# A two-layer hybrid encoder on one core: feed-forward on the input without the norm's factor, its low parts made by VectorE, the gate half scaled by Pool

## The chip, the cores and the metric

One core of one Trainium2 chip runs the whole kernel. The metric is the device time of one execution in microseconds; the kernel before has a median of 3319.37 us over three runs.

## The reference, cut to what matters

The input, 16 meta tokens and 512 tokens of 1024 channels, passes through two layers. Each layer is a half-step feed-forward, a mixing stage, and a second half-step feed-forward, so that there are four feed-forwards in all. Each sub-layer has an RMS norm ahead of it and one behind it:

```
def _rms_norm(x, g):
    y = xf * lax.rsqrt(jnp.mean(xf * xf, axis=-1, keepdims=True) + NORM_EPS)
    return y * g

def _swiglu(x, w_in, w_out):
    gate, up = jnp.split(x @ w_in, 2, axis=-1)
    return (jax.nn.silu(gate) * up) @ w_out

x = x + 0.5 * _rms_norm(_swiglu(_rms_norm(x, g_pre), w_in, w_out), g_post)
```

`w_in` is 1024 x 5632 (gate and up, 2816 each), `w_out` is 2816 x 1024. The norm's factor, 1/sqrt(mean + EPS), is one number per token. Because only the gate half passes through a nonlinear function, a factor per token left out of the up half multiplies the whole output of that token, and the norm behind removes it, but for its EPS.

## The kernel before, in words

Activations lie with channels on the partitions and tokens along the free dimension: `h` is 128 x 8 x 528. Every product of fp32 numbers is made of three fp32r matmuls: each operand is split in a high part (a copy in fp32r) and a low part (operand minus high part), and high x high, high x low and low x high are summed. So each 128 x 1024 piece of weights needs a high part (ScalarE, line 754) and a low part (a subtraction on VectorE, line 932, or on Pool in two instructions, line 636) before TensorE can use it.

A feed-forward is `phase_ffn` (line 534). It runs in this order.

- **The lead** (`Lead`, lines 340 to 477) finishes the norm behind the sub-layer before: VectorE scales `fo` (line 447) and adds it to `h` (line 450), one of eight channel blocks at a time. ScalarE makes `u_high` = h x gain (line 372) and the squares (line 375), VectorE `u_low` (line 442). The product of the first classical units is computed in the same loop (lines 706 to 719), from h x gain without the norm's factor. The factor `rs` is ready only after the last block: its sums (TensorE, line 417), a reciprocal (line 459) and a root (line 380).
- **The classical units**: the first 2 of 11 pairs of 128-wide blocks (NC = 2) are computed plainly, in four units each (lines 653 to 669), numbered 0 to 7. VectorE multiplies what comes out by `rs`, gate and up (`evac`, line 875), ScalarE applies silu (line 786), VectorE multiplies the two (line 889). Pool makes the low parts of these weights (lines 642 to 645).
- **The pairs 2 to 10** use Strassen's seven products, named A11, A22, A12, S2, S1, S3, S4 in their order on TensorE (`product`, line 671), with the input split in four quarters B11, B21, B22 and B12 and combined in four sums and differences T1 to T4. The inputs to these products are h x gain x rs, made by VectorE (`normalised`, line 894) in the storage of `hidden`, and then split again in high and low parts (`combo_high`, line 797, on ScalarE; `combo_low`, line 904, on VectorE). Every engine runs its queue in order, and the order is written out by hand. In pair p ScalarE has: the high part of product 3's weights; silu of the pair before, over both halves at once (`silu_pair`, line 790, called at line 848); then `s1`, a copy of the bank of A11 (lines 833 to 837); then high parts again. TensorE's third product, A12, accumulates in that bank and waits for `s1` (line 684). VectorE has, at the beginning of pair p: the last two sums of pair p-1 (`c21`, line 956, and `c12`, line 960), a weight's low part, and the product `hidden` of gate and up (line 966).
- **The output product** has 24 units of 8 or 6 weight blocks (line 729), whose low parts Pool makes (line 646). The high and low parts of the hidden tiles 0 to 19 are made during the last pair, those of 20 and 21 after it. `Out` (line 495) copies the result, scales it by the gain and sums its squares for the norm behind.

A ring of R = 4 buffers holds weights and their two parts; a transfer of new weights waits for the low part that last read the buffer (`free`, line 603).

Of the kernel before, what the change touches and what calls it, by code (L numbers as in the profile page):

```python
# [99 lines left out]
def build_program(nc, x, meta_tokens, norm_gain, ffn_w_in, ffn_w_out, w_in, rw_mu, rw_w0, rw_w_up,  # L100
# [4 lines left out]
    with ctx:  # L105
# [234 lines left out]
        class Lead:  # L340
# [6 lines left out]
            def __init__(self, st, ring, pre, banks, later):  # L347
                self.ring, self.pre, self.later = ring, pre, later
                self.rq = sb(st, "rq", [P, 2, 8])
                self.idle = PS[:, banks[2], 0:P]  # L350
# [11 lines left out]
            def scalar(self, act, between=None):  # L362
                nc.scalar.activation(self.rq[:, 0], ones[:, 0:8], ACT.Sqrt).then_inc(S("table"), 1)
# [14 lines left out]
                if self.later:  # L378
                    act.wait_ge(S("recip"), 2)
# [41 lines left out]
            def factor(self, v, own, x):  # L421
# [3 lines left out]
                rq = self.rq[:, x]  # L425
                sums = PS[:, self.bank if x else POST_BANK]
                nc.vector.tensor_scalar(rq[:, 0:full], sums[:, 0:64 * full:64], 1.0 / D_MODEL, EPS, ALU.mult, ALU.add)
                own(nc.vector.tensor_scalar(rq[0:m, full:full + 1], sums[0:m, 64 * full:64 * full + 1], 1.0 / D_MODEL,
                                            EPS, ALU.mult, ALU.add))
                nc.vector.reciprocal(rq, rq).then_inc(S("recip"), 1)  # L430

            def vector(self, v):
                own = Chain(v, S("norm_own"))
                v.wait_ge(S("table"), 1)
# [18 lines left out]
                if self.later:  # L453
                    low(KD - 1)
                v.wait_ge(S("h_summed"), KD)
                if self.later:
                    own(nc.vector.tensor_scalar(halves(rs[:]), self.wide_sums, 1.0 / D_MODEL, EPS, ALU.mult, ALU.add))
                    v.sem_inc(S("sums_read"), 1)
                    nc.vector.reciprocal(rs[:], rs[:]).then_inc(S("recip"), 1)
# [19 lines left out]
        def phase_post_norm(st):  # L479
            lead = Lead(st, None, None, (4, 6, 0), False)  # L480
# [14 lines left out]
        class Out:  # L495
# [6 lines left out]
            def __init__(self, st, gain, scale, done, cut):  # L502
                self.gs = sb(st, "gs", [P, KD])
                self.gain, self.scale, self.done, self.cut = gain, scale, done, cut
# [18 lines left out]
            def add(self, v):  # L523
                for m in range(1, KD - 1):
                    v.wait_ge(S("out_squares"), m + 1)
                    if m == 1 and self.cut.t0:
# [3 lines left out]
                    t = slice(self.cut.t0, T)  # L530
                    nc.vector.tensor_tensor(ssq[:, 2, t], ssq[:, 2, t] if m > 1 else ssq[:, 0, t], ssq[:, m % 2, t],  # L531
                                            ALU.add).then_inc(S("added"), 1)

        def phase_ffn(l, which, pre, gain, cut):

            with ExitStack() as st:
# [8 lines left out]
                ON_POOL = ()  # L545
# [9 lines left out]
                out = Out(st, gain, 0.5, S("unit_done"), cut)  # L555
                lead = Lead(st, [cc[:, 0, 0], cc[:, 0, 1]], pre, (6, 4, 0), True)
# [9 lines left out]
                by_pool = [True] * (4 * NC) + [j in ON_POOL for p in range(NC, NP) for j in range(7)] + [True] * NOUT  # L566
# [9 lines left out]

                def combo(e, h):

                    x = more[:, e, h] if e < 3 else flat((uh, ul)[h][:])[:, 2 * T * (e - 3):2 * T * (e - 2)]
                    return blocks(x[:, 0:4 * n2])  # L580

                plain = lambda x: flat(hid[:])[:, (4 + 2 * x) * T:(4 + 2 * x) * T + 4 * n2]
                OF = {B11: 0, B21: 2, B22: 3, T1: 4, T3: 5, T2: 6, T4: 7}
# [15 lines left out]

                with nc.Block() as block:  # L600
                    @block.sync
                    def _(sp):
# [9 lines left out]

                        for i in range(NP):
                            for q in range(2):
                                if i:
                                    free(i, q)
# [2410 lines left out]
```

## Time and profile before

| | |
|---|---|
| median of 3 runs (lowest, highest) | 3319.37 us (3317.99, 3324.27) |
| the profiled execution: its own time, its span | 3330.05 us, 3328.3 us |
| its mean granted TensorE clock | 0.978 |
| TensorE busy with matmuls | 3184.1 us (96%) |
| VectorE busy | 1905.9 us (57%) |
| ScalarE busy | 1350.7 us (41%) |
| Pool busy | 809.1 us (24%) |

The span runs from the first to the last instruction; the profiled execution's own time is 1.75 us longer. Busy time is the time in which at least one instruction of the engine runs. "Idle before" a group is the time for which the engine did nothing ahead of its instructions, with the instruction that ended the wait behind an arrow. The granted clock is a share of full speed: 1.00 is 2.4 GHz, 0.50 is 1.2 GHz.

The four feed-forwards begin at about 14, 1275, 1668 and 2920 us of the span. In the rows of the trace a time is the start in us from the span's start, followed by the duration in us.

### The profile page before, as it was taken

What the parts mean: (1) busy time and instruction counts of PE and PEld (TensorE: products, weight loads), DVE (VectorE), ACT (ScalarE), POOL (GpSimd) and SP (SyncE); (2) the same over time, 40 slices, a digit from 0 to 9 for tenths busy, and PEclk for the clock granted to TensorE, in tenths of its full rate; (3) what the DMA queues carried; (4) which work ended last, traced back from release to release, by engine and by line L of the source; (5) the groups of instructions that cost most, each with busy time, mean ns of one, the idle gap of its engine ahead of it and who ended that gap; (6) DMA issues with size and microseconds to landing.
All of it is one profiled execution on the core that took longest, in us unless ns stands there. A gap on an engine that the chain in (4) does not pass through costs nothing. (4 is left out here: it accounts for less than half of the span.)

```text
span 3328.3 us, 68766 instructions
## 1 busy us (share of the span) xinstructions
PE 3184.1 (96%) x29414; PEld 2957.0 (89%) x29414; DVE 1905.9 (57%) x2852; ACT 1350.7 (41%) x2277; POOL 809.1 (24%) x618
## 2 busy tenths in 40 slices
PE   8999999999999999999989999999999999989997
PEld 8999999987788999899989999999777778879986
DVE  7884055445767336886078831454467663378832
ACT  3444252224554333444245442523245553335541
POOL 4004335110012443003330043352100125420052
PEclk9999999999999999999999999999899999999999
DMA  3333222002121332333123332220021213223331
GB/s 103 102 102 94 61 75 68 12 3 64 45 52 32 93 93 71 94 109 99 56 94 101 107 89 62 64 62 12 12 61 45 52 42 95 80 82 107 117 91 49
DMA packets 369995, 237.30 MB, mean 71 GB/s; under 512 B 16510, under 2 KB 368012, under 8 KB 369692
## 3 DMA queue, kind: packets, MB, share of 16 engines
q1 hardware_dynamic: 369692, 232.91, 24.3%
q8 instruction: 233, 3.82, 0.5%
q14 instruction: 70, 0.57, 0.1%
HBM read 230.50 MB, written 2.10 MB: 70 GB/s over the span
## 5 line engine op out<-in xcount | busy, mean ns | idle before, releaser
L636 POOL TENSOR_TENSOR W_low<-W,W_high 128x512 fp32r<-128x512 f32 (+1 forms) x256 | 339.4, 1350 | 1192.3 <-ACT W_high L754 1191.8
L155 PE MATMUL PS<-u_high,dW_high 128*128 128x264 f32 (+1 forms) x1344 | 410.1, 305 | 12.9 <-POOL dW_low L2103 8.4
L157 PE MATMUL PS<-u_high,dW_low 128*128 128x264 f32 (+1 forms) x1344 | 386.5, 288 | 0.0
L156 PE MATMUL PS<-u_low,dW_high 128*128 128x264 f32 (+1 forms) x1344 | 386.0, 287 | 0.0
L155 PE MATMUL PS<-u_high,W_high 128*128 128x264 f32 (+1 forms) x1152 | 363.0, 315 | 15.1 <-POOL W_low L636 10.1
L754 ACT ACTIVATE W_high<-W 128x1024 fp32r<-128x1024 f32 (+1 forms) x236 | 241.2, 1027 | 322.6 <-PE PS L157 200.0
L156 PE MATMUL PS<-hidden_low,W_high 128*128 128x264 f32 (+1 forms) x1232 | 369.6, 300 | 0.0
L157 PE MATMUL PS<-u_high,W_low 128*128 128x264 f32 (+1 forms) x1152 | 357.2, 310 | 0.0
L700 PE MATMUL PS<-u_high,W_high 128*128 128x264 f32 (+1 forms) x1152 | 327.4, 284 | 8.3 <-DVE cc L944 8.3
L701 PE MATMUL PS<-u_low,W_high 128*128 128x264 f32 (+1 forms) x1152 | 327.4, 284 | 0.0
L702 PE MATMUL PS<-u_high,W_low 128*128 128x264 f32 (+1 forms) x1152 | 327.3, 284 | 0.0
L155 PEld LDWEIGHTS PS<-u_high,dW_high 128*128 128x128 f32 (+1 forms) x1344 | 257.2, 191 | 37.2 <-issue 18.5
L700 PE MATMUL PS<-u_more,W_high 128*128 128x264 f32 (+1 forms) x864 | 248.3, 287 | 20.9 <-DVE W_low L932 20.9
L531 DVE TENSOR_TENSOR ssq<-ssq 128x528 f32<-128x528 f32 (+1 forms) x36 | 32.3, 897 | 404.9 <-ACT ssq L519 404.9
L156 PEld LDWEIGHTS PS<-u_low,dW_high 128*128 128x128 f32 (+1 forms) x1344 | 257.3, 191 | 1.9
L157 PEld LDWEIGHTS PS<-u_high,dW_low 128*128 128x128 f32 (+1 forms) x1344 | 256.3, 191 | 0.0
L156 PE MATMUL PS<-u_low,W_high 128*128 128x264 f32 (+1 forms) x816 | 256.0, 314 | 0.0
L702 PE MATMUL PS<-u_more,W_low 128*128 128x264 f32 (+1 forms) x864 | 248.3, 287 | 0.0
L701 PE MATMUL PS<-u_more,W_high 128*128 128x264 f32 (+1 forms) x864 | 247.8, 287 | 0.0
L155 PEld LDWEIGHTS PS<-u_high,W_high 128*128 128x128 f32 x1152 | 218.1, 189 | 32.4 <-POOL W_low L636 11.2
L156 PEld LDWEIGHTS PS<-hidden_low,W_high 128*128 128x128 f32 x1232 | 231.6, 188 | 7.8
L2103 POOL TENSOR_TENSOR dW_low<-dW,dW_high 128x512 fp32r<-128x512 f32 x102 | 170.6, 1682 | 258.9 <-ACT dW_high L2098 258.7
(445 smaller groups left out, 8528.6 us busy)
## 6 DMA issues: line engine op xcount, KB each, us to landing
W<-in_ffn_w_in SPq DMA_DIRECT2D x176, 512.0 KB, 5.3
dW<-in_w_in SPq DMA_DIRECT2D x172, 256.0 KB, 2.9
W<-in_ffn_w_out SPq DMA_DIRECT2D x64, 512.0 KB, 4.1
W<-in_w_in SPq DMA_DIRECT2D x80, 256.0 KB, 3.0
W<-in_ffn_w_out SPq DMA_DIRECT2D x32, 384.0 KB, 3.4
W<-in_w_branch SPq DMA_DIRECT2D x48, 256.0 KB, 2.8
W<-in_w_out SPq DMA_DIRECT2D x32, 256.0 KB, 2.8
xt<-in_x SPq DMA_DIRECT2D x4, 512.0 KB, 5.4
```

Of the source, the lines that this page charges most:

```text
L155: nc.tensor.matmul(dst, wh, xh, start=first, stop=False)
L156: nc.tensor.matmul(dst, wh, xl, start=False, stop=False)
L157: return nc.tensor.matmul(dst, wl, xh, start=False, stop=final)
L531: nc.vector.tensor_tensor(ssq[:, 2, t], ssq[:, 2, t] if m > 1 else ssq[:, 0, t], ssq[:, m % 2, t], ALU.add).then_inc(S("added"), 1)
L636: ins = g.tensor_tensor(dst, src, high.bitcast(F32), ALU.subtract)
L700: nc.tensor.matmul(dst, wh, xh, start=OPENS[j] and k == 0, stop=False, skip_group_check=True)
L701: nc.tensor.matmul(dst, wh, xl, start=False, stop=False, skip_group_check=True)
L702: last = nc.tensor.matmul(dst, wl, xh, start=False, stop=k == 3, skip_group_check=True)
L754: copy = lambda dst, src: nc.scalar.activation(dst, src, ACT.Copy)
L2103: g.tensor_tensor(self.WL[:, r], self.W[:, r], self.WH[:, r].bitcast(F32), ALU.subtract).then_inc(S("d_split"), 1)
```

## The change

- The seven products of pairs 2 to 10 take h x gain without the factor. The quarters B11, B21 and B22 are now read from `u_high` and `u_low` as the lead made them, so they are not made again; only T1 to T4 are split in high and low parts. The eight unscaled blocks that the sums T1 to T4 need are made by ScalarE (`plain_parts`) between the lead's loop and the root, in place of the eight `normalised` on VectorE.
- In pairs 2 to 10 Pool multiplies the gate half by `rs`, 128 x 2 x 528 elements in one instruction, after `c11`, `c12`, `c21` and `c22` of that pair, and `silu_pair` waits for that. The up half is not scaled. The last pair's multiplication stands in Pool's queue ahead of the low parts of the output's weights.
- In the classical units VectorE multiplies only the gate by `rs`; the up half is read from PSUM by the product itself.
- The low parts of the classical units' weights, and of the first two output units, go from Pool to VectorE.
- The weights of pair 0 come in eight transfers of half the size, the first block's first.
- The low and high parts of the hidden tiles are placed elsewhere in the last pair: four each at its products 2, 4, 5 and 6, and 16 to 19 after it.
- Since the output is now larger by 1/rs, the EPS of the norm behind is multiplied by the mean of the squares (`mean`) and added to the sum of the output's squares, in one VectorE instruction more per feed-forward; the fixed EPS of that norm becomes 0.
- VectorE no longer waits at the beginning of a `Lead` for ScalarE's first table function.

The place of `silu_pair` in ScalarE's queue, between the high part of product 3 and the copy `s1`, is not changed, nor are the waits of A12 or the sums of a pair.

```
-            def scalar(self, act, between=None):
-                nc.scalar.activation(self.rq[:, 0], ones[:, 0:8], ACT.Sqrt).then_inc(S("table"), 1)
+            def scalar(self, act, between=None, after=None):
+                nc.scalar.activation(self.table[:], ones[:, 0:8], ACT.Sqrt)
...
-            def vector(self, v):
+            def vector(self, v, between=None):
                 own = Chain(v, S("norm_own"))
-                v.wait_ge(S("table"), 1)
...
                 for k in range(KD):
                     own(nc.vector.tensor_tensor(fo[:, k], fo[:, k], self.spread, ALU.mult))
+                    if between:
+                        between(k)
...
+                if self.mean is not None:
+                    v.wait_ge(S("out_squares"), 1)
...
+                    nc.vector.scalar_tensor_tensor(out=ssq[:, 2, t], in0=self.mean[:, t], scalar=KD * EPS,
+                                                   in1=ssq[:, 0, t], op0=ALU.mult, op1=ALU.add
+                                                   ).then_inc(S("mean_added"), 1)
...
-                by_pool = [True] * (4 * NC) + [j in ON_POOL for p in range(NC, NP) for j in range(7)] + [True] * NOUT
+                by_pool = [False] * (NIN + 2) + [True] * (NOUT - 2)
...
+                QUADRANT = {B11: (slice(0, 4), first_half), B21: (slice(4, 8), first_half),
+                            B22: (slice(4, 8), second_half), T3: (slice(0, 4), second_half)}
...
+                both_factors = rs[:, t0:T].unsqueeze(1).broadcast_to([P, 2, T - t0])
+                SPLIT_AT = {2: 0, 4: 1, 5: 2, 6: 3}
...
+                        for s in range(2):
+                            for q in range(2):
+                                for t in range(2):
+                                    c = t * D_FF + s * P
+                                    sp.dma_start(quarter(s, q)[:, t], wi[:, 4 * q:4 * q + 4, c:c + P]
+                                                 ).then_inc(landed[2 * q + t] if s else S(f"first_landed{q}"), 16)
...
-                        for i in range(NC):
-                            for s in range(2):
-                                for q in range(2):
-                                    by_set(classical(i, s, q), quarter(s, q))
+                        for p in range(NC, NP):
+                            for name in ("c11", "c12", "c21", "c22"):
+                                g.wait_ge(S(name), p - NC + 1)
+                            g.tensor_tensor(cc[:, 0, :, t0:T], cc[:, 0, :, t0:T], both_factors, ALU.mult
+                                            ).then_inc(S("scaled"), 1)
...
                         def silu_pair(p):
-                            act.wait_ge(S("c12"), p - NC + 1)
-                            act.wait_ge(S("c21"), p - NC + 1)
-                            act.wait_ge(S("c22"), p - NC + 1)
-                            act.wait_ge(S("c11"), p - NC + 1)
+                            act.wait_ge(S("scaled"), p - NC + 1)
                             nc.scalar.activation(cc[:, 0, :, t0:T], cc[:, 0, :, t0:T], ACT.Silu).then_inc(S("silu"), 1)
...
+                        def plain_parts():
+                            for k in range(KD):
...
+                                nc.scalar.activation(dst[:, :, k % 4 * n2:k % 4 * n2 + n2], two(h[:, k, t0:T]), ACT.Copy,
+                                                     scale=lead.gain(k)).then_inc(S("plain"), 1)
...
-                            tt(cut.of(cc[:, 1, s]), ps(1), cut.of(rs[:]), ALU.mult).then_inc(dve_evac, 1)
...
+                            tt(cut.of(hid[:, 2 * i + s]), PS[:, 4 * s + 2:4 * s + 2 + cut.a, 0:cut.n], cut.of(cc[:, 0, s]),
+                               ALU.mult).then_inc(S("hidden"), 1)
+
+                        def classical_low(n):
+                            i, s, q = n // 4, n // 2 % 2, n % 2
+                            v.wait_ge(S("high"), n + 1)
+                            tt(part_of(WL, n % R, n), quarter(s, q), part_of(WH, n % R, n).bitcast(F32), ALU.subtract
+                               ).then_inc(S("low_dve"), 1)
```

## Rows read from the trace of the kernel before

**Rows 1.** TensorE's waits over the whole span (us in total, times, longest us)

```profile
PE PS L700 <- DVE W_low L932: 20.9, 4, 5.9
PE PS L161 <- POOL W_low L636: 11.9, 4, 3.5
...
PE PS L155 <- POOL W_low L636: 10.1, 4, 3.1
...
PE PS L700 <- DVE cc L944: 8.3, 4, 2.3
```

**Rows 2.** Stretches on TensorE: from:to, length, busy, granted clock, DMA share, GB/s

```profile
24.00:94.00 70.00, 62.46 (x440) 0.90 0.25 79
271.00:275.00 4.00, 3.92 (x19) 0.57 0.09 27
1285.00:1354.00 69.00, 60.02 (x438) 0.93 0.25 77
1677.00:1747.00 70.00, 61.01 (x443) 0.93 0.25 81
1923.00:1927.00 4.00, 3.40 (x15) 0.57 0.01 4
2930.00:3000.00 70.00, 62.36 (x263) 0.90 0.28 89
```

**Rows 3.** ScalarE in order of time, at the beginning of one pair

```profile
175.88 1.09 ACT L795 ACTIVATE cc<-cc 128x1056 f32<-128x1056 f32 x1 [1.83 <-DVE cc L964]
176.88 0.60 ACT L754 ACTIVATE s<-PS 128x528 f32<-128x528 f32 x1
```

**Rows 4.** VectorE in order of time, in the same pair

```profile
175.15 0.70 DVE L964 TENSOR_TENSOR cc<-cc,PS 128x528 f32<-128x528 f32 x1
175.76 1.22 DVE L932 TENSOR_TENSOR W_low<-fo,W_high 128x1024 fp32r<-128x1024 f32 x1
```

**Rows 5.** TensorE in order of time: first matmuls of the third and fourth product

```profile
178.61 0.28 PE L700 MATMUL PS<-u_more,W_high 128*128 128x264 f32 x1
...
181.51 0.28 PE L700 MATMUL PS<-u_high,W_high 128*128 128x264 f32 x1
```

**Rows 6.** The beginning of the first feed-forward, all engines in order of time

```profile
21.43 2.95 POOL L636 TENSOR_TENSOR W_low<-W,W_high 128x512 fp32r<-128x512 f32 x2 [9.46 <-ACT W_high L754]
...
23.18 1.76 DVE L450 TENSOR_TENSOR h<-h,fo 128x528 f32<-128x528 f32 x1
...
24.52 0.36 PE L161 MATMUL PS<-u_high,W_high 128*128 128x264 f32 x1 [2.40 <-POOL W_low L636]
...
26.50 0.70 DVE L450 TENSOR_TENSOR h<-h,fo 128x528 f32<-128x528 f32 x1
...
82.25 2.01 ACT L754 ACTIVATE W_high<-W 128x1024 fp32r<-128x1024 f32 x2 [6.82 <-DMA W<-in_ffn_w_in]
```

**Rows 7.** Groups of Pool by shape: count | busy us, mean ns of one | idle before

```profile
L636 POOL TENSOR_TENSOR W_low<-W,W_high 128x256 fp32r<-128x256 f32 x32 | 23.5, 736 | 0.0
...
L1695 POOL TENSOR_TENSOR normed<-h,rs 128x528 f32<-128x528 f32 x16 | 20.8, 1300 | 23.0 <-POOLq L169 21.9
```

**Rows 8.** VectorE and Pool in order of time, 478 to 492 us

```profile
478.77 5.34 DVE L1381 TENSOR_TENSOR_SCAN rw_s<-rw_s 128x2112 f32<-128x2112 f32 x1 [0.22 <-DVE pj_rw L1367]
...
482.40 2.81 POOL L2103 TENSOR_TENSOR dW_low<-dW,dW_high 128x512 fp32r<-128x512 f32 x1 [2.70 <-ACT dW_high L2098]
...
486.74 3.23 DVE L1383 TENSOR_TENSOR rw_s<-rw_s 128x2112 f32<-128x2112 f32 x1
...
488.77 2.33 POOL L2103 TENSOR_TENSOR dW_low<-dW,dW_high 128x512 fp32r<-128x512 f32 x1 [1.02 <-ACT dW_high L2098]
```

**Rows 9.** TensorE after the second and fourth wait for L944; columns as in rows 2

```profile
1531.23 0.39 PE L700 MATMUL PS<-u_high,W_high 128*128 128x264 f32 x1 [2.00 <-DVE cc L944]
...
1532.00:1536.00 4.00, 4.00 (x35) 1.00 0.27 83
3171.00:3175.00 4.00, 4.00 (x36) 1.00 0.32 92
```

More of the change, by code:

```diff
@@ L340, in build_program, with __init__ @@
         class Lead:
-            def __init__(self, st, ring, pre, banks, later):
-                self.ring, self.pre, self.later = ring, pre, later
+            def __init__(self, st, ring, pre, banks, later, post_eps=EPS, mean=None):
+                self.ring, self.pre, self.later, self.post_eps, self.mean = ring, pre, later, post_eps, mean
                 self.rq = sb(st, "rq", [P, 2, 8])
+                self.table = sb(st, "table", [P, 8])
                 self.idle = PS[:, banks[2], 0:P]
@@ L378, in scalar @@
                 if self.later:
+                    if after:
+                        after()
                     act.wait_ge(S("recip"), 2)
@@ L495, in build_program, with __init__ @@
         class Out:
-            def __init__(self, st, gain, scale, done, cut):
+            def __init__(self, st, gain, scale, done, cut, mean=None):
                 self.gs = sb(st, "gs", [P, KD])
-                self.gain, self.scale, self.done, self.cut = gain, scale, done, cut
+                self.gain, self.scale, self.done, self.cut, self.mean = gain, scale, done, cut, mean
             def gains(self, v):
@@ L761, in classical_high @@
                             n = classical(i, s, q)
-                            for t in range(2):
-                                act.wait_ge(landed[2 * q + t], 16 * (i + 1))
+                            if i == 0 and s == 0:
+                                act.wait_ge(S(f"first_landed{q}"), 32)
+                            else:
+                                for t in range(2):
+                                    act.wait_ge(landed[2 * q + t], 16 * (i + 1))
                             ring(n)
@@ L985, in _ @@
                         combination(6, 3, 4)
-                        multiplied(0, 1)
                         v.wait_ge(S("combos"), 3)
                         combination(7, 2, 6)
-                        for e in range(3):
-                            combo_low(e)
-                        evac(1, 0)
+                        gate(0, 1)
+                        classical_low(6)
+                        classical_low(7)
+                        multiplied(0, 1)
+                        combo_low(T4)
+                        combo_low(T2)
+                        combo_low(T1)
                         sums(NC, S1)
+                        sums(NC, S2)
+                        gate(1, 0)
+                        sums(NC, S3)
                         multiplied(1, 0)
-                        sums(NC, S2)
-                        sums(NC, S3)
                         sums(NC, S4)
@@ L1041, in _ @@
                         c12(NP - 1)
+                        for k in range(16, KF - 2):
+                            hidden_low(k)
                         hidden(NP - 1)
@@ L2961, in ffn @@
             def ffn(which, gain, cut):
-                phase_ffn(l, which, G_NORM + KD * 4 * which, gain, cut)
+                phase_ffn(l, which, G_NORM + KD * 4 * which, gain, cut, EPS if which or l == 0 else 0.0)
             ffn(0, G_NORM + KD, WHOLE)
```

175 lines of the change are left out of this document (94 added, 81 removed).

## The prediction

> **What bounds the kernel now.** I read the page first: TensorE is busy for 96% of the span, so whatever does not shorten or lengthen its waits costs nothing. The change removes no matmul. The next view is therefore the list of TensorE's waits. Its four largest entries inside the feed-forwards, four waits each, are for low parts of weights made by VectorE (20.9 us), for low parts made by Pool (11.9 and 10.1 us) and for a sum of VectorE (8.3 us): 51.2 us in 16 waits [rows 1]. All four belong to the beginning of a feed-forward, but for the last, which falls in the last pair of blocks. The second thing to see is the granted clock of the same stretches [rows 2]: behind these waits it falls to its lower level, 1.2 GHz of 2.4. What was lost is (1 - granted share) x length: 7.0, 1.7, 4.8, 4.9, 1.7 and 7.0 us, together 27.1 us. Third, one pair of the steady part (20.4 us, nine in each of four feed-forwards) on ScalarE, VectorE and TensorE [rows 3 to 5]. There TensorE never waits; I read it for how late each helper may be.
>
> **What the change does at the beginning of a feed-forward.** The first low part takes Pool 2.95 us in two instructions, and TensorE starts at 24.52 after 2.40 us of idleness [rows 6]. Afterwards VectorE makes it in one instruction of 1.22 us [rows 4] and the first weights come in half-size transfers, so TensorE starts some 2.2 us earlier. VectorE also no longer runs against Pool: its addition of h took 1.76 us beside a Pool instruction and takes 0.70 without one [rows 6]. The eight products h x gain x factor leave VectorE for ScalarE, where they lie before the root of the sums; ScalarE was idle there. Three high and three low parts of the input are not made at all, because u_high and u_low now serve as they are. So the low parts of classical units 4 to 7 are done before TensorE comes to them, and the transfer of the first pair's weights, which was so late that ScalarE waited 6.82 us for it up to 82.25 [rows 6], is issued over 10 us earlier by my walk, as soon as the low parts of units 6 and 7 free the buffers. SP's queue gets four transfers more ahead of the parameter loads, which are needed only at the feed-forward's end. I take all twelve waits of the beginning as gone. In the last pair the low parts of the hidden tiles move behind the sum that the sixth product needs, so that wait (8.3 us in four) goes too.
>
> A wait costs 0.16 us more than the idle time listed, since a matmul lasts 0.28 us but its successor starts 0.12 us after it [rows 5]: (181.51 - 178.61)/24 = 0.12. Gain: 51.2 + 16 x 0.16 + 27.1 = 80.9 us. What is late next: 0.2 us at the first product; 0.5 at the fifth step of the lead, where VectorE has 1.2 us of a low part more; in the first pair the second product waits for the hidden tile made from the last classical unit (the gate product, table function and product, 0.70 each, start late behind three low parts: 4.2 us after the unit, with 2.9 of cover, so 1.3). With 0.1 at unit 3 that is 2.1 us in each of four. At the end of a feed-forward Pool's queue holds the last scaling ahead of the low parts of output unit 2. I walk it to 1.5 us too late, and half of these waits bring down the clock at 1.7 us each: 4 x 1.5 + 2 x 1.7 = 9.4. So 80.9 - 8.4 - 9.4 = 63. VectorE no longer waits for ScalarE's table at seven beginnings, 0.15 us each: 1. **Gain in all: 64 us.** The extra VectorE addition (mean times EPS, one per feed-forward, 0.7 us as its neighbours) lies beside output products; if TensorE did not cover it, it would cost 4 x 0.7.
>
> **What it adds in each pair.** Until now the gate half went from VectorE's last sum (175.15 to 175.85) straight to ScalarE: table function at 175.88, then in the same queue the copy of the first product, s1, from 176.88 to 177.48 [rows 3, 4]. The third product accumulates in the bank that this copy reads, and waits for it; it starts at 178.61 [rows 5], 1.13 us after the copy. The change puts Pool's multiplication between the sum and the table function, and leaves table function and copy in their order. Behind the waiting table function stand the copy and a weight's high part, and for the copy waits TensorE.
>
> Pool's instruction reads 128x1056. Undisturbed it took 1.30 us for 128x528 and 0.74 for 128x256 [rows 7], so 1056 take 1.30 + 528 x 0.56/272 = 2.39. But at 175.76 VectorE starts a low part from two SBUF operands, 1.22 us long [rows 4], 0.17 us before Pool can start. Two rows show what that does: Pool's 128x512 (1.27 by the same slope) took 2.81 with 1.71 us of such a VectorE instruction still to run, and 2.33 with 1.20 [rows 8]. It ends later by what is left less 0.15. Here 1.05 is left: 2.39 + 0.90 = 3.29. From both sides the price is 2.39 (no hindrance) to 3.6 (the whole 1.22 added, nothing overlapped); I take 3.29 as the rows nearest to it give it.
>
> Walk: sum done 175.85, Pool starts 175.93 and ends 179.22, the table function starts 0.14 later (the step that TensorE shows behind Pool at 24.52 [rows 6]), the copy 1.00 after it [rows 3] and ends 180.96; product three starts at 181.01, not 178.61. **2.4 us** are lost. They don't come back: VectorE's chain to the last sum hangs on TensorE's fifth product, so it shifts along and the next pair has the same offset. Pairs that have such a predecessor: 8 in each of 4 feed-forwards, 32. 32 x 2.4 = 77 us.
>
> The clock: four waits of about 2 us for VectorE's sum stood alone in a dense stretch. Behind the first and third of them the clock was 0.57 over 4 us [rows 2], behind the second and fourth it stayed at 1.00 [rows 9]. A fall costs 0.43 x 4 = 1.7 us. The new idle time is 2.4 - 0.16 = 2.24 us, so I take 0.6 falls per wait (bounds 0 and 1): 32 x 0.6 x 1.7 = 33 us.
>
> **Sum.** 77 + 33 - 64 = +46 us. The sum is made against the profiled execution (span 3328.3, time 3330.05, so 3376 for it); that run stood 10.7 us above the median of the three, to which the same difference is applied: 3319.4 + 46 = **3365 us**.
>
> **Rivals.** (a) *Faster*: Pool's multiplication runs undisturbed. On the page "SBUF — State Buffer" (section "SBUF: two separate sides") the Trainium skill says that whichever of the two engines starts first gets the shared port pair for the whole instruction; rows 8 agree for the case that VectorE is first. By that rule it is a race of 0.17 us here: if Pool starts first, VectorE waits instead, on which nothing hangs. Then 3.29 becomes 2.39, the loss per pair 1.5 us with 1.34 us idle, shorter than any wait of rows 9, so no falls: 32 x 1.5 = 48, and 48 - 64 = -16: 3303 us. The case turns at 64/32 = 2.0 us per pair, falls included. Against it speaks that VectorE's queue is back to back in every pair shown. Chance 0.17. (b) The waits of the beginning go and the pairs' do not come, because something I overlooked gives ScalarE the copy in time: -64, 3255 us. Both the wait for s1 and the order in ScalarE's queue stand in the code and in rows 3, so 0.05. (c) Every new wait brings the clock down: 77 + 55 - 64 = +68, 3387 us. 0.13. (d) The change does not do at the beginning what it should: VectorE, now with eight weight low parts more in its queue, becomes the late engine and only about half the gain comes: 110 - 30 = +80, 3399 us. For it: VectorE is behind by fractions of a microsecond in my walk. 0.07. My forecast keeps 0.58.
>
> **Numbers.** A measurement of this kernel can tell 0.2%, 6.6 us, from no change. Forecast, (c) and (d) are slower; (a) is faster in most of its spread, which reaches the band, as does the low edge of the forecast (1.5 to 2.7 us per wait, 0 to 1 falls). That makes faster 0.20, same 0.05, slower 0.75. The forecast alone spans 3335 to 3385. The range takes in (a)'s centre and (c), and just (d): 3300 to 3400.
>
> **What would show each step.** Right: a wait of TensorE for ScalarE's s1, 32 times, some 2.2 us each; Pool's multiplication 36 times near 3.3 us; pairs 22.8 us apart or 24.5 where the clock fell, in place of 20.4; no wait for W_low of more than 1 us; the first pair's first product some 12 us earlier. Wrong: Pool's multiplication at 2.4 (a), no wait for s1 (b), granted clock in the steady part above 0.98 or under 0.92 (a, c), waits for W_low of VectorE left at the beginning (d).

## The result: 2% slower, and the profile after

| | before | after |
|---|---|---|
| median | 3321.6 us (4 runs beside those of after) | 3389.2 us (4 runs, 3384.3 to 3396.2) |
| ratio to before | 1 | 1.0206, interval 1.0184 to 1.0228 |
| profiled execution: time, span | 3330.05, 3328.3 us | 3396.2, 3394.5 us |
| TensorE busy, mean granted clock | 96%, 0.978 | 95%, 0.972 |

The change costs 68 us by the medians and 66 us by the profiled executions. The forecast was 46 more, 3365 us, with a range of 3300 to 3400: direction and range held, the size was 22 us too small by the medians and 20 by the profiled executions, which the account below goes by.

The page after. TensorE's busy time does not say how much work it has (no matmul was added); the waits do.

```profile
span 3394.5 us, 68689 instructions
PE 3216.8 (95%) x29414; PEld 2982.9 (88%) x29414; DVE 1836.7 (54%) x2837; ACT 1354.3 (40%) x2297; POOL 807.7 (24%) x574
```

TensorE's waits after (us in total, times, longest), the ones inside the feed-forwards:

```profile
PE PS L733 <- ACT s L787: 69.5, 32, 2.3
PE PS L155 <- POOL W_low L671: 8.8, 4, 2.7
...
PE PS L733 <- DVE hidden L927: 3.8, 4, 1.1
...
PE PS L161 <- DVE W_low L933: 2.5, 4, 0.6
...
PE PS L733 <- DVE W_low L967: 1.0, 1, 1.0
```

The four entries of [rows 1] are gone: 51.2 us in 16 waits have become 7.3 us in nine small ones (hidden, and VectorE's low parts). In their place stand 32 waits for the copy s1, 69.5 us, and four for Pool at output unit 2, 8.8 us, the first output unit whose low part Pool makes.

One pair after, in order of time (start, duration, engine, line, operation, idle time before it and what ended it); VectorE, Pool, ScalarE, TensorE:

```profile
172.35 0.70 DVE L1005 TENSOR_TENSOR cc<-cc,PS 128x528 f32<-128x528 f32 x1
172.96 1.22 DVE L967 TENSOR_TENSOR W_low<-fo,W_high 128x1024 fp32r<-128x1024 f32 x1
173.18 3.33 POOL L677 TENSOR_TENSOR cc<-cc,rs 128x1056 f32<-128x1056 f32 x1 [19.52 <-DVE cc L1005]
...
176.53 1.08 ACT L828 ACTIVATE cc<-cc 128x1056 f32<-128x1056 f32 x1 [5.23 <-POOL cc L677]
177.52 0.59 ACT L787 ACTIVATE s<-PS 128x528 f32<-128x528 f32 x1
...
178.17 0.39 PE L733 MATMUL PS<-u_high,W_high 128*128 128x264 f32 x1 [2.14 <-ACT s L787]
```

This is the chain of the forecast with its numbers: the sum ends at 173.05, Pool holds the gate half until 176.51, the table function follows and then the copy, which does not need the scaling at all but stands behind it in ScalarE's queue. Before, from the sum's start to the third product it was 178.61 - 175.15 = 3.46 us [rows 4, 5]; now it is 178.17 - 172.35 = 5.82, so 2.36 us more against the 2.4 forecast.

The clock, in the windows of nine pairs each (from:to, length, TensorE busy, granted clock, DMA share, GB/s), and then over 4 us behind two single waits of 2.14 us, those that end at 178.17 and at 155.32:

```profile
100.00:280.00 180.00, 162.86 (x1248) 0.94 0.30 93
1377.00:1556.00 179.00, 161.87 (x1241) 0.94 0.29 92
1786.00:1966.00 180.00, 162.86 (x1248) 0.94 0.29 92
3052.00:3229.00 177.00, 158.94 (x1239) 0.93 0.30 93
...
178.20:182.20 4.00, 4.00 (x20) 0.57 0.00 1
...
155.40:159.40 4.00, 4.00 (x33) 1.00 0.01 4
```

The missing 0.06 of 180 us is 10.8 us, six falls of 1.7 us in a feed-forward. Counted one by one in the trace's record of the granted clock, 25 of the 32 waits had the lower level behind them and 7, with the same idle time, had not. The 7 are not scattered. In the first feed-forward the fall began 0.48 us after the end of the first wait (106.56) and 0.00 after that of the second (130.94), and behind the third (155.32) there was none; then it began 0.56 and 0.08 us after, and there was none again. The second and third feed-forward show the same drift. In the fourth, where the pairs are some 23.9 us apart, the first wait was spared and at all the others the fall began within 0.05 us of the wait's end. In the first three feed-forwards pairs are 22.85 us apart without a fall and about 24.4 with one.

### The profile page after: what moved, and what is told of

The parts are those of the page before. It is cut to its first block and busy times, and to the rows that moved or that the text cites. A ratio compares the mean times of both kernels' runs of the same rounds, so it can differ in the third digit from the quotient of the medians.

```text
span 3394.5 us, 68689 instructions
## 1 busy us (share of the span) xinstructions
PE 3216.8 (95%) x29414; PEld 2982.9 (88%) x29414; DVE 1836.7 (54%) x2837; ACT 1354.3 (40%) x2297; POOL 807.7 (24%) x574
## 5 line engine op out<-in xcount | busy, mean ns | idle before, releaser
L733 PE MATMUL PS<-u_high,W_high 128*128 128x264 f32 (+1 forms) x1152 | 349.1, 303 | 70.5 <-ACT s L787 69.5
L677 POOL TENSOR_TENSOR cc<-cc,rs 128x1056 f32<-128x1056 f32 (+1 forms) x36 | 123.9, 3443 | 1061.3 <-DVE cc L1005 1061.3
L155 PE MATMUL PS<-u_high,W_high 128*128 128x264 f32 (+1 forms) x1152 | 362.2, 314 | 5.0 <-ACT vg L2588 1.9
L157 PE MATMUL PS<-u_high,W_low 128*128 128x264 f32 (+1 forms) x1152 | 356.0, 309 | 0.0
L734 PE MATMUL PS<-u_low,W_high 128*128 128x264 f32 (+1 forms) x1152 | 344.5, 299 | 0.0
L735 PE MATMUL PS<-u_high,W_low 128*128 128x264 f32 (+1 forms) x1152 | 343.8, 298 | 0.0
L733 PEld LDWEIGHTS PS<-u_high,W_high 128*128 128x128 f32 x1152 | 235.4, 204 | 77.6 <-ACT s L787 76.1
L967 DVE TENSOR_TENSOR W_low<-fo,W_high 128x1024 fp32r<-128x1024 f32 x144 | 175.4, 1221 | 196.1 <-ACT W_high L787 196.1
L671 POOL TENSOR_TENSOR W_low<-W,W_high 128x512 fp32r<-128x512 f32 (+1 forms) x176 | 212.7, 1232 | 201.9 <-ACT W_high L787 201.9
L156 PE MATMUL PS<-u_low,W_high 128*128 128x264 f32 (+1 forms) x816 | 254.9, 312 | 0.0
L733 PE MATMUL PS<-u_more,W_high 128*128 128x264 f32 (+1 forms) x864 | 244.4, 283 | 3.8 <-DVE hidden L927 3.8
L734 PE MATMUL PS<-u_more,W_high 128*128 128x264 f32 (+1 forms) x864 | 244.2, 283 | 0.0
```

Source lines behind the costliest of these rows:

```text
L155: nc.tensor.matmul(dst, wh, xh, start=first, stop=False)
L156: nc.tensor.matmul(dst, wh, xl, start=False, stop=False)
L157: return nc.tensor.matmul(dst, wl, xh, start=False, stop=final)
L671: ins = g.tensor_tensor(dst, src, high.bitcast(F32), ALU.subtract)
L677: g.tensor_tensor(cc[:, 0, :, t0:T], cc[:, 0, :, t0:T], both_factors, ALU.mult).then_inc(S("scaled"), 1)
L733: nc.tensor.matmul(dst, wh, xh, start=OPENS[j] and k == 0, stop=False, skip_group_check=True)
```

## The account: where 66 us came from

A span splits into three parts: TensorE's idle time, which is the span less its busy time on the page; the loss by the clock, which is half of the time at the lower level within the span that isn't idle anyway; and the rest, its work at full speed. The clock's parts are summed over the trace's clock record. All in us:

| | before | after | difference | forecast |
|---|---|---|---|---|
| idle | 144.3 | 177.7 | +33.4 | 71.7 - 51.2 + 8.4 + 6 = +34.9 |
| time at the lower level (of it idle) | 148.7 (20.0) | 188.1 (10.1) | | |
| loss by the clock | 64.4 | 89.0 | +24.7 | 33 + 3.4 - 27.1 = +9.3 |
| rest | 3119.7 | 3127.7 | +8.0 | 5.1 - 2.6 - 1 = +1.5 |
| span | 3328.3 | 3394.5 | +66.2 | +46 |

The forecast's column sorts its terms the same way: 77 is 71.7 of idle time and 32 x 0.16 of restart. The idle time is right, and by the listed waits too: 69.5 + 8.8 + 7.3 - 51.2 = 34.4. Fifteen of the missing 20 us are the clock. Six to seven are in the rest: I had 1.5 there; the waits more (147 idle stretches of over 0.15 us instead of 117, at 0.16 each) explain 4.8 of the 8.0, and 3 are not placed. The idle time gives back 1.5.

## Experiments

All ratios are to the kernel before, run on the same chip in turns. The median of before itself was 3321.6 us beside after and 3324.4 to 3330.0 beside the experiments. So differences to after, which are given by the medians, carry a few us of that; by the ratios they are larger (113 us in place of 106 in experiment 1, 62 for 58 in 3, 125 for 119 in 5). The line numbers of an experiment can differ by some from those of after.

### 1. Is it the order in ScalarE's queue?

The table function moves behind the copy s1 and the next high part; Pool's multiplication stays.

```diff
-                                if j == 0 and p > NC:
+                                if j == 1 and p > NC:
                                     silu_pair(p - 1)
```

> The changed kernel with one call moved: ScalarE's table function of the pair before now stands behind the copy s1 and the next high part, not ahead of them. My theory (the whole loss is TensorE's 32 waits for that copy, 2.14 to 2.26 us idle each, and 25 falls of the clock behind them): no wait for s1 is left, Pool's multiplication still takes 3.3 us, and the time falls by 32 x 2.3 + 25 x 1.7 = 117 us to about 3272 us, some 50 us below the kernel before. Rival (Pool at work beside VectorE is what costs, by holding up VectorE's low parts): most of the loss stays, over 3350 us, with waits for W_low of VectorE.

Measured: 3282.8 us, ratio 0.9865 (0.9846 to 0.9884), 106 us below after, where 117 were expected. The waits for s1 are gone without a rest. One pair, by the engines' rows:

```profile
161.95 1.22 DVE L967 TENSOR_TENSOR W_low<-fo,W_high 128x1024 fp32r<-128x1024 f32 x1
...
162.17 3.33 POOL L677 TENSOR_TENSOR cc<-cc,rs 128x1056 f32<-128x1056 f32 x1 [17.14 <-DVE cc L1005]
...
162.15 0.62 ACT L787 ACTIVATE s<-PS 128x528 f32<-128x528 f32 x1 [1.86 <-PE PS L735]
162.66 1.05 ACT L787 ACTIVATE W_high<-fo 128x1024 fp32r<-128x1024 f32 x1
...
163.74 2.84 DVE L967 TENSOR_TENSOR W_low<-fo,W_high 128x1024 fp32r<-128x1024 f32 x1 [0.57 <-ACT W_high L787]
...
165.53 1.09 ACT L828 ACTIVATE cc<-cc 128x1056 f32<-128x1056 f32 x1 [1.82 <-POOL cc L677]
```

Pool's instruction is as slow as in after, 3.33 us, and costs nothing, because only the table function waits for it and ScalarE has 1.82 us to spare. The copy starts as soon as TensorE is done with its bank. So the loss in the pairs is one position in one queue: there the multiplication by itself is free. Only the last one of each feed-forward still costs, at output unit 2 (10.5 us of waits; experiment 6).

### 2. Pool or the multiplication?

VectorE does the same multiplication, right behind its last sum; Pool's loop is gone, the table function stays ahead of the copy.

```diff
+                        def scale_pair(p):
+                            for name in ("c11", "c12", "c21", "c22"):
+                                v.wait_ge(S(name), p - NC + 1)
+                            tt(cc[:, 0, :, t0:T], cc[:, 0, :, t0:T], both_factors, ALU.mult).then_inc(S("scaled"), 1)
```

> The changed kernel with the gate half scaled by VectorE right behind its last sum, ScalarE's order left as it is. My theory: the table function starts some 1.35 us later than before the change in place of 3.4, of which 1.1 are covered, so the waits for s1 shrink to 0.1 to 0.4 us each with no fall of the clock, and Pool's low parts at the end of a feed-forward no longer stand behind a scaling: 3389 - 117 + 11 - 17 = about 3266 us. Rival (any scaling ahead of the table function costs about the same, whoever makes it): above 3350 us.

Measured: 3275.8 us, 0.9843 (0.9811 to 0.9876), 10 us above the expected 3266. Eight waits for s1 are left, all short:

```profile
PE PS L728 <- ACT s L782: 1.7, 8, 0.2
```

The path from the sum to the copy still holds a multiplication, but one of VectorE, 1.26 us long (Pool's is 3.33), with no hand-over to another engine. It fits into the cover that TensorE's second product gives. So a scaling ahead of the table function does not cost by itself either; the loss takes both, a late step of 3.33 us and a copy that stands behind it.

### 3. What does VectorE's neighbouring instruction cost?

VectorE may start its next low part only when Pool has scaled, so Pool runs alone.

```diff
+                                        v.wait_ge(S("scaled"), p - NC)
```

> The changed kernel where VectorE starts its low part only when Pool's multiplication is done; ScalarE's order left as it is. My theory: Pool's multiplication falls from 3.33 to 2.4 us, the waits for s1 from 2.14 to about 1.25 us idle, 32 x 0.9 = 29 us less, and waits of this length bring no fall of the clock, 43 us less: about 3317 us, no different from the kernel before. If waits of 1.25 us bring the clock down as well: about 3360 us. Rival (Pool takes 3.3 us for this shape whatever VectorE does): 3389 us or more.

Measured: 3331.4 us (10 runs), 1.0020 (1.0008 to 1.0032), 58 us below after and 14 above the expected 3317. Pool's group, first after, then here (count: minimum/median/maximum in ns), and the waits here:

```profile
L677 POOL TENSOR_TENSOR cc<-cc,rs x36: 2947/3326/4672, 101.6 to 3244.7; 128x1056 f32<-128x1056 f32 x27, 128x1024 f32<-128x1024 f32 x9
```

```profile
L677 POOL TENSOR_TENSOR cc<-cc,rs x36: 2393/2482/4670, 100.4 to 3182.2; 128x1056 f32<-128x1056 f32 x27, 128x1024 f32<-128x1024 f32 x9
...
PE PS L733 <- ACT s L787: 43.0, 32, 1.7
PE PS L155 <- POOL W_low L671: 11.0, 4, 3.0
```

Alone Pool takes 2.48 us, with VectorE's low part running 3.33: a hindrance of 0.85, forecast 0.90; the undisturbed part was put at 2.39. Each wait became 1.34 us in the mean (1.30 to 1.71), and none of the 32 was followed by a fall of the clock. That is rival (a) come true, whose price was 48 us for the waits, and they cost 43.0 + 32 x 0.16 = 48. Its total of 3303 is 28 us below the 3331 measured, and what it has too low is not the waits but the gain of 64 us that it set against them: experiment 5 shows how much of that there was, and the last scaling's wait takes 11.0 us here with three falls. Split as in the account above, against after: idle time 177.7 - 155.6 = 22, loss by the clock 89.0 - 40.9 = 48, less 8 of the rest, which is longer here; together 62.6, the difference of the two profiled executions. So the last 0.85 us of Pool's instruction cost twice as much by the clock as by themselves.

The Trainium skill, "SBUF — State Buffer" (section "SBUF: two separate sides"), calls the port pair that the two engines share an exclusive lock, held for a whole instruction by whoever starts first. The rows agree for VectorE's subtraction of two SBUF operands, in both directions. With VectorE first, Pool ended 2.33 us after VectorE's end (176.51 against 174.18 in after; 165.50 against 163.17 in experiment 1). With Pool's already at work, in experiment 1, VectorE's low part at 163.74 took 2.84 us instead of 1.22, and ended 1.08 behind Pool's end.

### 4. The multiplication added to the kernel before

Before, with a tile of ones by which Pool multiplies the gate half ahead of the table function: the disputed step without the rest of the change.

```diff
+                        for p in range(NC, NP):
...
+                            g.tensor_tensor(cc[:, 0, :, t0:T], cc[:, 0, :, t0:T],
+                                            unity[:, t0:T].unsqueeze(1).broadcast_to([P, 2, T - t0]), ALU.mult
+                                            ).then_inc(S("scaled"), 1)
...
+                            act.wait_ge(S("scaled"), p - NC + 1)
```

> The kernel before with Pool's instruction alone added at the same place, a multiplication by a tile of ones, so that nothing else is changed. My theory: 32 waits for s1 of 2.1 us, falls behind most of them, and a wait for Pool's low part at each feed-forward's end: 3322 + 74 + 43 + 10 = about 3450 us; what separates it from the changed kernel, some 60 us, is the gain of the other parts. Rival (the change's other parts bring nothing, or the loss is due to their moved queues): about 3390 us.

Measured: 3490.5 us, 1.0488 (1.0470 to 1.0506), 40 us beyond the expectation. The waits for s1 came as in after; most of the surplus stands in the second line:

```profile
PE PS L709 <- ACT s L763: 71.6, 32, 2.4
PE PS L155 <- POOL W_low L637: 45.4, 8, 9.8
PE PS L709 <- DVE W_low L938: 17.5, 4, 4.5
PE PS L709 <- DVE cc L950: 10.7, 5, 3.0
```

In the kernel before Pool makes the low parts of all output units, and the last scaling now stands ahead of the first of them: three waits of 8.5 us and one of 9.8, 35 of the 45.4, where I had expected 10 in all for this place. The change gives the first two output units to VectorE, and there the wait behind the last scaling is 8.8 us. That looks like a detail of the diff, and by these two traces it spares 26 us of idle time once Pool scales; no run takes it back by itself. My prediction did not mention it, because nothing of it shows in the trace of before. Of the 32 waits for s1, 2.19 to 2.45 us long here, 21 were followed by a fall, not 25.

### 5. No scaling at all

After without Pool's loop; the table function waits for the four sums themselves. The gate half of pairs 2 to 10 is left unnormalised, and so is everything that hangs on it.

```diff
-                            act.wait_ge(S("scaled"), p - NC + 1)
+                            act.wait_ge(S("c12"), p - NC + 1)
...
```

> The changed kernel without the scaling of the gate half in pairs 2 to 10 (so these hidden tiles are computed from a gate half that is not normalised), ScalarE's order left as it is. It measures what all the other parts bring by themselves. My theory: neither the 32 waits for the copy nor the four at the feed-forwards' ends, 3322 - 57 = about 3265 us, the same as the version with the copy first and the tail mended. If the scaling also costs in ways other than its waits: clearly below 3260 us.

Measured: 3270.4 us, 0.9831 (0.9807 to 0.9855). This is the whole gain of the rest of the change, 54 to 56 us, with no price for the scaling in it; 57 were expected. My 64 was made of the same parts less 9.4 for the wait behind the last scaling (the tail), which here is absent: 73 would have been the number for this kernel, so it was overrated by 17 us. Against the profiled execution of before (56 us) the same split says where: idle time fell by 40.2, where I had 42.8; the loss by the clock by 23.0 against my 27.1, 4 of which lay in idle time and were counted twice; and the rest grew by 7.1, where I had a fall of 3.6. That last part is 11 of the 17, and I have no row for it.

### 6 and 7. Versions that keep the gain

Experiment 6 is experiment 1 with the last pair's scaling behind Pool's low part of output unit 2; experiment 7 is 2 and 1 together.

```diff
-                        for p in range(NC, NP):
+                        for p in range(NC, NP - 1):
+                            scale_pair(p)
...
+                            if u == 3:
+                                scale_pair(NP - 1)
```

> The first experiment (copy ahead of the table function) with one more move: in Pool's queue the low parts of output unit 2 stand ahead of the last pair's scaling, not behind it. My theory: the four waits at the feed-forwards' ends for Pool's low parts (10.5 us idle in that run, each with a fall of the clock) come from this order alone and go: 3283 - 10.5 - 4 x 1.9 = about 3265 us. Rival (Pool is simply behind there, because VectorE's hidden low parts hold it up, and the wait moves to output unit 3 or to hidden tiles 20 and 21): 3280 us or more.

> VectorE scales the gate half as in the second experiment, and ScalarE's copy stands ahead of the table function as in the first. My theory: the scaling on VectorE already left only 1.7 us of waits for the copy, so this brings 2 us at most against the second experiment: 3270 to 3276 us, and neither the waits at the feed-forwards' ends nor those for the copy appear. Rival (VectorE's queue, now 1.25 us per pair fuller, becomes late elsewhere): new waits for VectorE and 3285 us or more.

Measured: 3263.9 us, 0.9805 (0.9786 to 0.9824), where 3265 was expected, and 3265.0 us, 0.9814 (0.9795 to 0.9834), 5 us under its range. Of experiment 1, where the last scaling stayed first in Pool's queue, first the wait, then the last scaling and what it pushed back:

```profile
PE PS L155 <- POOL W_low L671: 10.5, 4, 3.0
...
267.46 4.67 POOL L677 TENSOR_TENSOR cc<-cc,rs 128x1056 f32<-128x1056 f32 x1 [20.07 <-DVE cc L1005]
272.08 10.89 POOL L671 TENSOR_TENSOR W_low<-W,W_high 128x512 fp32r<-128x512 f32 x8
```

And of experiment 6, the same place:

```profile
268.56 2.82 POOL L677 TENSOR_TENSOR cc<-cc,rs 128x1056 f32<-128x1056 f32 x1 [4.40 <-DVE cc L1010]
271.34 3.47 POOL L671 TENSOR_TENSOR W_low<-W,W_high 128x512 fp32r<-128x512 f32 x2
```

The wait has gone, and with it four falls: 10.5 + 4 x 1.7 = 17, measured 19 between the medians. Experiment 6 is the best kernel of the study, 65 us faster than before and 125 us faster than after (133 by the ratios); 7 cannot be told from it.

### 8 and 9. Two moves of the beginning taken back

Both on experiment 1. In 8 Pool makes the eight low parts of the classical units again, in 9 the first weights come in whole transfers.

```diff
-                by_pool = [False] * (NIN + 2) + [True] * (NOUT - 2)
+                by_pool = [True] * (4 * NC) + [False] * (NIN - 4 * NC + 2) + [True] * (NOUT - 2)
```

> The first experiment with the low parts of the eight classical weight pieces given back to Pool, everything else as changed. Question: what of the gain of some 60 us at the beginnings comes from moving these low parts. If only the first of them matters (Pool needs 2.95 us where VectorE needs 1.22, and TensorE waits for that): 4 x 1.8 us and the falls behind them, 3283 + 12 = about 3295 us. If the move as a whole made the gain, and the eight products taken off VectorE did nothing: waits for Pool's low parts at units 4 to 7 and for the first pair come back, 3340 us.

> The first experiment with the weights of pair 0 in four whole transfers again. If the smaller first transfers let TensorE start earlier: the first high part is made at about 6.2 us after the feed-forward's beginning again in place of 5, TensorE's first product starts 1.1 us later in each of four, 3283 + 5 = 3288 us, more if the longer wait brings the clock down. If the transfers were hidden behind VectorE's first blocks anyway: 3283 us, no difference.

Measured: 3284.4 us, 0.9867 (0.9847 to 0.9887), and 3284.2 us, 0.9867 (0.9848 to 0.9887), against 0.9865 with both in place. Waits of the first classical unit, of 8 and then of 9 (2.5 in four in after):

```profile
PE PS L161 <- POOL W_low L671: 7.1, 4, 2.1
```

```profile
PE PS L161 <- DVE W_low L923: 6.1, 4, 1.8
```

Each wait is there, 4.6 us and 3.6 us longer in all, and the total does not move by what a measurement can tell; the intervals leave room for some 9 us either way. Neither is what the beginning gained by, and run 8 went past both numbers written ahead of it.

### 10. The move of the last pair alone

The kernel before, with the high and low parts of the hidden tiles placed as in after.

```diff
-                                if p == NP - 1 and j >= 2:
-                                    for k in range(4 * (j - 2), 4 * (j - 1)):
+                                if p == NP - 1 and j in SPLIT_AT:
+                                    for k in range(4 * SPLIT_AT[j], 4 * SPLIT_AT[j] + 4):
```

> The kernel before with the new places of the hidden tiles' high and low parts in the last pair and nothing else. My theory: the wait of the last pair's sixth product for VectorE's sum (8.3 us idle in four, two falls of the clock) goes: -8.3 - 0.6 - 3.4 = -12 us, about 3310 us. Rival (the moved parts come late for the output product or delay Pool's first low parts): no gain or a loss, 3322 us or more.

Measured: 3316.6 us (10 runs), 0.9976 (0.9965 to 0.9987), 8 us faster. The wait for the sum (8.3 us [rows 1]) is gone, a small one came, and the largest entry of before is untouched:

```profile
PE PS L701 <- DVE W_low L935: 20.9, 4, 6.1
...
PE PS L155 <- DVE cc L951: 1.4, 4, 0.7
```

My account had 8.3 + 0.6 + 2 x 1.7 = 12 for this part, at the upper edge of the measured interval of 4 to 12 us.

### 11 and 12. What the beginning gains by

On experiment 6: in 11 VectorE makes the eight products h x gain that the change put on ScalarE; 12 is 11 with the classical low parts on Pool as well.

```diff
-                        lead.scalar(act, first_high, plain_parts)
+                        lead.scalar(act, first_high)
...
+                        for k in range(KD):
...
+                            nc.vector.tensor_scalar(dst[:, :, k % 4 * n2:k % 4 * n2 + n2], two(h[:, k, t0:T]), lead.gain(k),
+                                                    None, ALU.mult).then_inc(S("plain"), 1)
```

> The version with the copy first and the tail mended (3264 us), but the eight unscaled blocks of the input are made by VectorE behind the reciprocal, where the normalised ones were, not by ScalarE ahead of the root. If it is this move that opens the beginning: 8 blocks of 0.4 to 0.7 us put the sums T4 to T3 and everything behind them 3 to 6 us later, the low parts of units 6 and 7 and the first pair's transfers too, and TensorE waits 2 to 5 us at the first pair with a fall of the clock: 3264 + 15 to 30 us, about 3285. If the gain comes from not making the quarters and from VectorE being free of Pool's hindrance: within 5 us of 3264.

> The mended version (3264 us) with both of the moves undone that brought nothing when undone alone: VectorE makes the eight unscaled blocks, and Pool makes the low parts of the eight classical weight pieces. If the two moves stand in for each other (together VectorE's eight blocks run against Pool's subtractions and each is two to three times as long, which puts the sums, the low parts of units 4 to 7 and the first pair's transfers late): waits for W_low at units 6 and 7 or at the first pair return, 2 to 5 us in each of four, falls with them, 3285 to 3310 us. If what opened the beginning is that the three quarters are not made again and up halves not copied: within 6 us of 3264, apart from the first product's wait for Pool.

Measured: 3268.0 us, 0.9826 (0.9805 to 0.9847), and 3279.7 us, 0.9850 (0.9829 to 0.9871), against 0.9805 in experiment 6: 7 us for the one, 15 for both. The 15 are clear; the 7 are not, since the intervals of 11 and 6 overlap (TensorE's idle time in the profiled executions is 3.8 us longer in 11). Of the numbers written ahead of 11, the one for a move that does not matter, within 5 us of 3264, fits; ahead of 12, the 3280 measured lies between the two. The waits inside the beginning with both undone:

```profile
PE PS L161 <- POOL W_low L671: 5.7, 4, 2.1
PE PS L745 <- DVE hidden L939: 4.3, 4, 1.1
PE PS L161 <- ACT u_high L373: 3.8, 5, 0.9
...
PE PS L155 <- DVE cc L934: 3.2, 4, 1.2
PE PS L745 <- DVE W_low L980: 2.1, 4, 0.7
```

The 20.9 us of [rows 1] don't come back: both engines have these products and low parts again as before, and the kernel is still 1.5% faster than before. Some 8 us of it are the last pair's (experiment 10). What is left for the rest is that three quarters of the input are no longer multiplied by the factor and split anew, and that the factor stands no more ahead of the sums; but also that VectorE no longer scales the up half of the classical units, and that the half-size first transfers stayed in both runs. That is argued from what these runs leave over; no run puts any of this back here, so which of it opens the beginning isn't shown.

## Why the prediction was right, and where it was short

- **The new wait** [rows 3 to 5] was right in place, number and size: 32 times, 2.14 us (2.26 in the eight of the fourth feed-forward) against 2.24. Experiments 1 and 5 show it to be the loss: without it the kernel is 106 and 119 us faster than after.
- **Pool's price** [rows 7, 8] was right at 3.29 against 3.33, both parts by a few hundredths: 2.48 for 2.39, 0.85 for 0.90. Experiment 3 separates them. That the multiplication "runs undisturbed" (a) did not happen: 24 of the 36 took 3.32 or 3.33 us, eight in the narrower fourth feed-forward 2.95 to 3.24, the four last ones 4.54 to 4.67; no undisturbed 2.4 to 2.5 is among them.
- **Falls of the clock** is the term mis-sized. I took 0.6 per wait from four waits, two of which had a fall [rows 2, 9]; it was 25 of 32, 0.78: (25 - 19) x 1.7 = 10 us of the 20, and the tail brought two falls more. Four cases were too few for a term that is multiplied by 32, and more of them might not have helped: waits as long were followed by a fall in 21 of 32 in experiment 4, and the drift seen above says that the share hangs on how far apart the waits are, which the change itself moved. No run varies that by itself. Rival (c), a fall at every wait, gave 3387 and was nearer to the 3389 measured than my forecast, but by luck: its 32 falls did not happen. The forecast's mechanism did, with 0.78, a larger tail and a smaller gain elsewhere.
- **The tail** was underrated: four waits of 2.2 us with a fall each instead of 1.5 with one in two, (8.8 - 6) + 2 x 1.7 = 6 us. I gave the last scaling the price of every other. It is 4.67 us:

```profile
295.68 1.32 DVE L978 TENSOR_TENSOR hidden_low<-hidden,u_high 128x528 fp32r<-128x528 f32 x2
296.92 1.32 DVE L978 TENSOR_TENSOR hidden_low<-hidden,u_low 128x528 fp32r<-128x528 f32 x2
...
295.89 4.67 POOL L677 TENSOR_TENSOR cc<-cc,rs 128x1056 f32<-128x1056 f32 x1 [23.40 <-DVE cc L1005]
300.52 8.23 POOL L671 TENSOR_TENSOR W_low<-W,W_high 128x512 fp32r<-128x512 f32 x5
...
304.15 0.39 PE L155 MATMUL PS<-u_more,W_high 128*128 128x264 f32 x1 [1.91 <-POOL W_low L671]
```

  These rows are from after, VectorE, Pool and TensorE in the last pair. The very subtractions that the change moved behind the sum (to save the 8.3 us of [rows 1]) now lie upon Pool's scaling.
- **The beginning** was right in its waits and partly wrong in its reasons. TensorE in after, at its first product, at the first matmul of the first pair, which it reaches without a wait, and at the second product of that pair:

```profile
22.71 0.36 PE L161 MATMUL PS<-u_high,W_high 128*128 128x264 f32 x1 [0.63 <-DVE W_low L933]
...
76.67 0.28 PE L733 MATMUL PS<-u_high,W_high 128*128 128x264 f32 x1
...
80.78 0.39 PE L733 MATMUL PS<-u_more,W_high 128*128 128x264 f32 x1 [1.03 <-DVE hidden L927]
```

  And in before, the first matmul of the first pair:

```profile
88.80 0.56 PE L700 MATMUL PS<-u_more,W_high 128*128 128x264 f32 x1 [4.66 <-DVE W_low L932]
```

  Forecast were 0.2 and 1.3 us of idle time; the first product comes 1.8 us earlier than in [rows 6], where I had 2.2, and the first pair 12 us, as forecast. Of the causes I named, Pool's slow first low parts (experiment 8) and the half-size transfers (experiment 9) are worth nothing that can be measured, VectorE's relief of the eight products at most some 7 us, with overlapping intervals (experiment 11). And what these parts are worth together was put too high: experiment 5 shows 54 to 56 us where my terms make 73, most of it in the part that is neither idle time nor clock.
- **Rivals.** (b) is the result of experiment 5, not of the change. (d), VectorE late, has nothing for it: TensorE's longest wait for it in a feed-forward is 1.1 us. The rival I did not have is that of experiment 4, the last scaling ahead of all output low parts, which the change's own companion move averts.

## What to carry to other kernels

An instruction on an in-order queue that gets a later operand delays everything behind it, so ask of a new step whose queue the waiting consumer stands in, and put what others wait for ahead of it: here moving one call behind a copy was worth 106 us, while letting the slow step run undisturbed was worth 58. Work moved onto Pool is to be priced together with every VectorE instruction that will run beside it, place by place, since the last of nine equal instructions took 1.3 us longer than the others. And for a wait that repeats 32 times, four examples don't give the share that brings the clock down: bound it by none and all, and carry both ends into the range.

## What the runs showed of the hardware

- Idle time of 1.30 to 1.71 us in a dense stretch was followed by a lower granted clock in 0 of 32 cases (experiment 3), of 2.14 to 2.26 us in 25 of 32 (after), of 2.19 to 2.45 us in 21 of 32 (experiment 4). Which of the 32 of after were spared does not go by their length (the waits that end at 155.32 and 178.17 are both 2.14 us), but in a row: in the first three feed-forwards the fall began some 0.5 us earlier from one wait to the next, counted from the wait's end, and after it had come down to the end one wait was spared.
- Pool's multiplication of 128x1056 took 2.48 us alone, 3.33 beside one VectorE instruction of two SBUF operands that had begun 0.2 us before it, and 4.67 with four such instructions back to back (two groups of 1.32 us), the first of which had begun 0.21 us before it. It ended 2.33 us after the end of VectorE's instruction in the one case and 2.32 after the end of the last in the other (300.56 against 298.24): Pool did not get in between them, and the row of four held it up like one long instruction.
